# Twenty of 24 head units of a two-block model as seven products each, with sums by GpSimd, and their loads on the weight queue

## What is computed

```python
h = _rmsnorm(x, g_mix_pre)
proj = h @ w_in                                     # 2048 x 16832
q = _rope(proj[..., OFF_DA_Q:OFF_DA_K].reshape(B, S, DA_HEADS, 2, DA_HEAD_DIM), pos)
k = _rope(proj[..., OFF_DA_K:OFF_DA_V].reshape(B, S, DA_HEADS, 2, DA_HEAD_DIM), pos)
v = proj[..., OFF_DA_V:OFF_RW].reshape(B, S, DA_HEADS, DA_V_DIM)
o_a = _diff_attention(q, k, v, lam, da_subln_g, lambda_init)      # 8 heads
o_b = _rwkv7(proj[..., OFF_RW:OFF_GATE], ...)                     # a recurrence in chunks of 64
gates = sigmoid(proj[..., OFF_GATE:] + b_gate)
mix = (gates[..., :D] * (o_a @ w_branch_a) + gates[..., D:] * (o_b @ w_branch_b)) @ w_out
```

## Time and profile before

| | us |
|---|---|
| median of 3 runs | 3943.13 (3942.73 to 3945.35) |
| the profiled execution | 3944.76, of which the span from first to last instruction is 3943.0 |

### The profile page before, as it was taken

How to read it: one execution, slowest core, us unless ns; L and a number is a source line. 1 busy time by engine, 2 the same in 40 slices (tenths; PEclk the granted TensorE clock), 3 DMA queues, 4 the chain that set the end, 5 groups by cost and what they waited for, 6 DMA issues and landing times.

```text
span 3943.0 us, 66861 instructions
## 1 busy us (share of the span) xinstructions
PE 3817.8 (97%) x28964; PEld 3559.2 (90%) x28964; DVE 1799.8 (46%) x3157; ACT 592.8 (15%) x1314; POOL 1308.9 (33%) x737
## 2 busy tenths in 40 slices
PE   8999999999999999999999999989898899999997
PEld 7888888889888999999999998878697899999997
DVE  1344426582223613111135446552522788778544
ACT  0333311110111111000000000232402211111001
POOL 0000000046511774777750000001340677775000
PEclk9999999999999999999999999999999999999999
DMA  6565664447664543444444554427242344444442
GB/s 230 212 217 215 217 231 162 160 166 237 211 196 171 206 161 148 165 165 168 169 166 162 171 193 165 170 108 204 75 169 83 115 172 171 171 171 150 172 159 77
DMA packets 122133, 673.37 MB, mean 171 GB/s; under 512 B 31872, under 2 KB 38144, under 8 KB 91248
## 3 DMA queue, kind: packets, MB, share of 16 engines
q1 hardware_dynamic: 87200, 580.29, 41.0%
q0 software_dynamic: 11104, 42.89, 3.5%
q10 hardware_dynamic: 23536, 45.92, 3.3%
HBM read 615.80 MB, written 53.25 MB: 170 GB/s over the span
## 4 chain that ended last, share of the span: by engine, by line
PE 93%; DVE 3%; ACT 2%; DVEq 1%; issue 1%; ACTq 0%; DMA 0%; POOL 0%; POOLq 0%
PE product_bank L576 53%; PE product_bank L635 26%; PE product_bank L413 3%; PE mixer_bank L784 1%; PE mixer_bank L800 1%; ACT xT L902 0%; PE mixer_bank L1334 0%; PE mixer_bank L1348 0%; PE mixer_bank L1165 0%; PE product_bank L2416 0%; PE mixer_bank L2378 0%; PE mixer_bank L2344 0%; PE mixer_bank L1157 0%; DVE arena L832 0%; PE mixer_bank L1323 0%
## 5 line engine op out<-in xcount | busy, mean ns | idle before, releaser
L635 PE MATMUL product_bank<-hT,weight_ring 128*128 128x256 f32 x2688 | 593.6, 380 | 1.6 <-ACT out_stage L674 1.6
L635 PEld LDWEIGHTS product_bank<-hT,weight_ring 128*128 128x128 f32 x2688 | 508.8, 190 | 75.3 <-issue 7.2
L576 PE MATMUL product_bank<-hT,weight_ring 128*128 128x128 f32 x4160 | 521.9, 276 | 14.5 <-DVEq L1808 5.8
L576 PEld LDWEIGHTS product_bank<-hT,weight_ring 128*128 128x128 f32 x4160 | 494.0, 193 | 20.2 <-DVEq L1808 6.0
L576 PE MATMUL product_bank<-arena,weight_ring 128*128 128x128 f32 x3168 | 394.6, 275 | 0.0
L543 POOL TENSOR_TENSOR arena<-weight_ring 128x1024 f32<-128x1024 f32 x88 | 209.6, 2382 | 528.3 <-PE product_bank L576 284.8
L576 PEld LDWEIGHTS product_bank<-arena,weight_ring 128*128 128x128 f32 x3168 | 374.8, 192 | 0.6
L611 DVE TENSOR_TENSOR arena<-product_bank,arena 128x128 f32<-128x128 f32 x126 | 36.7, 291 | 712.4 <-PE product_bank L576 712.4
L2804 DVE SCALAR_TENSOR_TENSOR arena<-arena 128x256 f32<-128x256 f32 x176 | 320.1, 1857 | 16.5 <-ACT arena L2769 13.2
L546 POOL TENSOR_TENSOR weight_ring<-weight_ring 128x1024 f32<-128x1024 f32 (+1 forms) x142 | 315.5, 2222 | 0.0
L576 PE MATMUL product_bank<-hT,arena 128*128 128x128 f32 x2096 | 257.1, 276 | 1.4 <-DVE hT L532 1.4
(11 more groups left out here) (506 smaller groups left out, 5435.8 us busy)
## 6 DMA issues: line engine op xcount, KB each, us to landing
weight_ring<-in_weights SPq DMA_DIRECT2D x213, 2048.0 KB, 8.0
weight_ring<-in_weights SPq DMA_DIRECT2D x128, 512.0 KB, 5.6
weight_ring<-in_weights SPq DMA_DIRECT2D x64, 384.0 KB, 5.3
units<-out_stage ACTq DMA_DIRECT2D x87, 256.0 KB, 7.7
rwkv_keep<-arena ACTq DMA_DIRECT2D x16, 1282.0 KB, 6.3
arena<-rwkv_keep SPq DMA_DIRECT2D x8, 1280.0 KB, 11.8
arena<-units POOLq DMA_DIRECT2D x33, 256.0 KB, 3.4
arena<-units SPq DMA_DIRECT2D x25, 256.0 KB, 9.0
```

The source lines that it names most:

```text
L576: mm = pe.matmul(bank[:, at * P:at * P + P], lhs[:, j, :], rhs[:, j, :], start=g == 0 and n in (0, 3) and j == 0, stop=g == n_groups - 1 a ...
L635: mm = pe.matmul(psg[b][:, half * T:half * T + T], lhs, rhs, start=k == 0, stop=k == 15)
```

## The change

The head units get two stage names: "heads0" for the first 4, still plain, and "heads" for the other 20, which become sevens in two groups, as the gates' units are. Their weights, their slots and their order stay. A v unit is stored by token, so it takes weights and source in the other places of the matmul (`turned`), and its recombination writes to the quadrants in another order.

GpSimd no longer loads anything for the heads. It waits for the last recurrence tile and sums for 20 + 16 units in one list (`early_sums_pool`), with the same buffers, though the buffers of both groups lie in `yT` for all "heads" units. ScalarE copies one of seven products and stores a unit one unit later, when VectorE has recombined it. VectorE recombines 20 units more, in its program behind the quarters in which a plain unit's would have stood empty.

SP loads the inverse's matrix behind the weights of the ninth head unit and the heads' q, k and v behind those given in `HEAD_LOADS_AT`. The loads of gates unit 4 have nothing behind them any more. The source is combined once, at the same place as before.

```diff
+HEADS_PLAIN = 4
+ORDER += [("heads0", u) for u in range(HEADS_PLAIN)] + [("heads", u) for u in range(24 - HEADS_PLAIN)]
+def turned(name, u):
+    return name in ("heads0", "heads") and head_and_part(name, u)[1] == 2
...
-                if n == UNIT_AT["gates", 4][0]:
-                    last_head_load(sp)
+                if n == UNIT_AT["heads0", 0][0] + 8:
+                    inverse_load(sp)
+                for h in HEAD_LOADS_AT.get(n - UNIT_AT["heads0", 0][0], ()):
+                    head_load(sp, h)
...
-        EARLY = ("gates",)
+        EARLY = ("heads", "gates")
...
+                        one, other = (rhs, lhs) if turned(name, u) else (lhs, rhs)
+                        mm = pe.matmul(bank[:, at * P:at * P + P], one[:, j, :], other[:, j, :],
...
-        def inv_pool(pool):
-            all_kept(pool)
-            pool.dma_start(inv_M, l_units).then_inc(sem("inverse_moved"), 16)
+        def inverse_load(sp):
+            all_kept(sp)
+            sp.dma_start(inv_M, l_units).then_inc(sem("inverse_moved"), 16)
...
-        def gates_sums_pool(pool):
-            for u in range(16):
+        def early_sums_pool(pool):
+            pool.wait_ge(sem("rw1_tile_done"), RW_TILES)
+            for n, unit in enumerate(SEVENTHS):
                 for g in range(2):
-                    if (u, g) == (6, 1):
+                    if (unit, g) == (("gates", BESIDE_DA), 1):
                         pool.wait_ge(sem("attn_head_done"), DA_HEADS)
-                    sum_gates(pool, u, g)
+                    sum_early(pool, n, g)
...
+        HEAD_LOADS_AT = {8: [0], 10: [1], 13: [2], 16: [3], 19: [4], 22: [5], 25: [6], 28: [7]}
+
+        def head_load(sp, h):
+            s = h % 2
+            if h >= 2:
+                sp.wait_ge(sem("attn_head_done"), h - 1)
+            for c in range(3):
+                unit = head_unit(h, c)
+                unit_stored(sp, *unit)
+                sp.dma_start(dain[:, s, c, :], row_of(*unit)).then_inc(sem(f"da_in{s}"), 16)
...
+        SEVENTHS = [("heads", u) for u in range(24 - HEADS_PLAIN)] + [("gates", u) for u in range(16)]
+
+        def sum_early(pool, n, g):
+            if n:
+                group_used(pool, *SEVENTHS[n - 1], g)
+            name, u = SEVENTHS[n]
+            sum_weights(pool, name, u, g, early_sums_of(name, u, g))
...
+        def early_product_act(act):
+            act.wait_ge(sem("rw1_tile_done"), RW_TILES)
+            for n, (name, u) in enumerate(SEVENTHS):
+                yield
+                yield
+                if n:
+                    store_early(act, n - 1)
+                yield
+                if n >= 2:
+                    seq = UNIT_AT[SEVENTHS[n - 2]][1]
+                    act.wait_ge(bank_free[seq % 4], seq // 4 + 1)
+                copy_first_act(act, name, u, gates_first[u % 2])
+                yield
...
+                if turned(name, u):
+                    sides = kept_.rearrange("p (h c n) -> p c h n", h=2, c=2)
+                    left, right = sides[:, 0, :, :], sides[:, 1, :, :]
+                else:
+                    left, right = kept_[:, 0:T], kept_[:, T:2 * T]
+                recombine_dve(dve, name, u, gates_first[u % 2], *gates_temps, left, right)
+                dve.drain().then_inc(sem("early_kept"), 1)
...
             rw1_pool(pool)
-            inv_pool(pool)
-            da_pool(pool)
-            gates_sums_pool(pool)
+            early_sums_pool(pool)
...
-            elsewhere = (None for _ in range(4 * 45))
-            dense = chain(elsewhere, gates_product_dve(dve))
+            elsewhere = (None for _ in PLAIN for _ in range(4))
+            dense = chain(elsewhere, early_product_dve(dve))
```

More of the change, by code:

```diff
@@ L53 @@
 ]
-STORED = ("rkv", "lora", "qk", "v", "gates", "mem_k", "mem_v", "sqk", "sv", "nq", "nkc", "nk", "nv", "ng")
+STORED = ("rkv", "lora", "heads0", "heads", "gates", "mem_k", "mem_v", "sqk", "sv", "nq", "nkc", "nk", "nv", "ng")
 class Stage:
@@ L87, with head_and_part, head_unit @@
 GROUPS = 6
+def head_and_part(name, u):
+    return divmod(u + (HEADS_PLAIN if name == "heads" else 0), 3)
+def head_unit(h, part):
+    k = 3 * h + part
+    return ("heads0", k) if k < HEADS_PLAIN else ("heads", k - HEADS_PLAIN)
+def turned(name, u):
+    return name in ("heads0", "heads") and head_and_part(name, u)[1] == 2
 def plan():
@@ L105, in plan @@
             first = home[name] + (u // shared) * max(1, int(slots))
+            if name in ("heads0", "heads"):
+                h, part = head_and_part(name, u)
+                first = (home["qk"] + h, home["qk"] + 8 + h, home["v"] + h)[part]
             here = len(loads)
@@ L590, in early_quarters @@
             for u in range(PLAN[name].units):
-                steps = unit_sevens(pe, name, u, lambda g: half(source_blocks(src), g), lambda g: sums(u, g),
+                steps = unit_sevens(pe, name, u, lambda g: half(source_blocks(src), g), lambda g: sums(name, u, g),
                                     lambda g: half(combined, g))
@@ L611, in recombine_dve @@
             dve.tensor_tensor(u2, X[:, P:2 * P], first, ALU.add)
-            dve.tensor_tensor(left[:, 0:P], X[:, 0:P], first, ALU.add)
+            left, right = (v if len(v.shape) == 3 else halves(v) for v in (left, right))
+            dve.tensor_tensor(left[:, 0, :], X[:, 0:P], first, ALU.add)
             dve.drain()
@@ L630, in unit_quarters @@
                 for k in range(16):
-                    if st.layout == "T":
+                    if st.layout == "T" and not turned(name, u):
                         lhs, rhs = w[:, k, half * P:half * P + P], src[:, k, :]
@@ L1488, in build @@
         LAM = small[:, 20:22]
[L1490 to L1505, removed]
+        HEAD_LOADS_AT = {8: [0], 10: [1], 13: [2], 16: [3], 19: [4], 22: [5], 25: [6], 28: [7]}
[7 more added lines that the diff above has]
+                sp.dma_start(dain[:, s, c, :], row_of(*unit)).then_inc(sem(f"da_in{s}"), 16)
         def da_head_in(eng, i, s):
[L1508 to L1511, removed]
+            eng.wait_ge(sem(f"da_in{s}"), 48 * i + 48)
         def da_pe(pe):
@@ L2816, in build @@
         RKV_GROUPS = [[("rkv", 8 * c + t) for c in range(3)] for t in range(8)]
-        HEAD_GROUPS = [[("qk", h), ("qk", 8 + h), ("v", h)] for h in range(DA_HEADS)]
+        PLAIN = [unit for group in RKV_GROUPS[1:] for unit in group] + [("heads0", u) for u in range(HEADS_PLAIN)]
         RW1_LEAD, DA_LEAD, RW2_LEAD = 4, 14, 6
@@ L2886, in _ @@
                 run(unit_quarters(pe, name, u, hT))
-            dense = chain(*(unit_quarters(pe, name, u, hT) for group in RKV_GROUPS[1:] + HEAD_GROUPS for name, u in group),
-                          early_quarters(pe, "gates", hT, early_combined, gates_sums_of),
+            dense = chain(*(unit_quarters(pe, name, u, hT) for name, u in PLAIN),
+                          *(early_quarters(pe, name, hT, early_combined, early_sums_of) for name in ("heads", "gates")),
                           quarters(pe, "branch_a", oaT, ready="attn_head_done", count=DA_HEADS))
@@ L2918, in _ @@
                 store_unit(act, name, u)
[L2919 to L2920 removed]
+            dense = chain(*(unit_store_quarters(act, name, u) for name, u in PLAIN), early_product_act(act), branch_a_act(act))
             beside(dense, rw1_act(act), beside_rw1, RW1_LEAD)
@@ L2958, in _ @@
             dve.drain()
-            combine_source_dve(dve, "gates", source_blocks(hT), early_combined)
+            combine_source_dve(dve, "heads", source_blocks(hT), early_combined)
             def heads_and_inverse():
```

45 lines of the change are left out of this document (16 added, 29 removed).

## The result

The changed kernel takes 3994.5 us (median of 4 runs, 3990.07 to 3999.3), the kernel before 3943.5 beside it: a ratio of 1.0127 (1.0115 to 1.0139), 1.3% slower. The forecast was 3975 with a range of 3932 to 4015. The profiled execution took 3995.7 us, its span 3993.8, so 50.8 us of span are to be found. Lines have moved: L576 is now L599 (sevens), L635 L659 (plain), L617 L641 (a recombination's last instruction), L1193 and L1196 (inverse) L1217 and L1220, L1574 L1591, L1581 L1598 (roped k), L1603 L1620 (softmax's last), L1610 L1627, L1524 L1541 (rotation), L1531 L1548 (scores), L1537 L1554 (transposes).

The account below looks back on a forecast made before the run. TensorE, busy 97%, bounds the kernel before; in the changed heads VectorE was to set the pace. From 3944.8 us: +31.5 for seven heads, 0 for lead, head 7 and loads, -1.6 to the median: 3975 us, range 3932 to 4015.

Parts of the forecast that it names:

- The rival that VectorE keeps up: Heads: sums fall into VectorE's rests, TensorE sets the pace; 3917 us, or 3934 with stalls; chance 0.20.
- the one that GpSimd is the bound: Heads: stretched sums take GpSimd 43.4 us a head, so no change, 3943 us; chance 0.09.
- the one of the queue: SP's loads: a head's load waits for a late store, weights behind come late; +54, 3971 us; chance 0.04.
- the forecast had 12: Heads: 12 VectorE instructions a head stretched by GpSimd's sums, 0.91 us each; ends 4 and 22.
- its own 32.3 us: VectorE's own work and short waits in a head before: 43.5 us less 11.2 of rest ahead of the reciprocal.
- the forecast had 48.0: Distance between heads: VectorE's 37.3 us plus 12 collisions of 0.91 is 48.2, rounded to 48.0.
- The price of 0.91: What a VectorE instruction loses beside a GpSimd sum: 1.67 us instead of 0.76 for 572 elements.
- the prediction's 4005 by that rule: Total if each collision cost VectorE a whole sum, 1.27 us and not 0.91: 30 us more.
- +31.5: Seven heads' term: 7 x 48.0 = 336.0 us, before 304.5.
- no term of the sum is about the clock: Lead and heads: the clock stood at 1.00, the upper level, so the sum gives it 0 us.
- 7 or 8: TensorE's lateness a head, in us: some 4 for rope, 2 for softmax, 1 to 2 for ScalarE behind recombinations.
- the 4.6 that was taken: Lead: TensorE's wait for first sums, between 0 and 8 us, taken as +4.6 to even the -4.6 gain.

Follow-up runs that it names:

- idle_sums: Kernel before with the changed loads, all head units plain, GpSimd making 20 units' sums on scratch nobody reads; 3974.5 us, ratio 1.0078.
- short_sums: Changed kernel with the head units' sums over 16 columns instead of 128 of each block; 3939.3 us, one run.
- loads_only: Kernel before with the inverse's and all heads' loads on SP, head units plain, no GpSimd sums in that stage; 3944.3 us, ratio 1.0001.
- placed: Changed kernel with VectorE's inverse steps only behind the softmax and its neighbours, none between reciprocal and rope; 3992.3 us, ratio 1.0121.
- early_inverse: Changed kernel with the first 8 head units plain and 20 of the inverse's 62 steps done in the lead; 3959.6 us, ratio 1.0040.
- front_inverse: Changed kernel with 12 head units plain, 20 inverse steps in the lead, 16 more in heads beside plain units; 3943.7 us, ratio 0.9999.
- front_placed: front_inverse with the inverse steps left for heads beside sums placed only behind the softmax; 3950.4 us, ratio 1.0015.
- placed8: early_inverse with the other 42 inverse steps placed only behind the softmax; 3960.1 us, ratio 1.0042.
- front_placed_after: front_placed with the inverse steps behind the recombination due at a head's step instead of ahead of it; 3936.1 us, ratio 0.9980.

## Why the prediction was right and wrong

**Direction and mechanism: right.** VectorE became what TensorE waits for, through the stretch of its own instructions and the recombinations. `idle_sums` shows the first without the second, `short_sums` the second without the first, and without the stretch the seven heads beat the old ones. The rival that VectorE keeps up is out (46 to 53 us apart, not 40 to 42). So are the one that GpSimd is the bound (TensorE waits 1.3 us for it) and the one of the queue (`loads_only`). The Trainium skill, Perfetto Trace Analysis, section Identifying the Most-Contended Engine, would have the engine with the highest occupancy relieved first, TensorE here (97%, and 90% by its weight loads, which is the measure that the page prefers). The runs show that the relief of 1.31 us a unit is lost when an engine that is busy 46% gets it as work in a fixed order.

**The account of a head: its terms right, its sum partly luck.** The seven heads have 92 stretched instructions, 13.1 a head, which cost 12.0 us; the forecast had 12, at 10.9. With its own 32.3 us and 5.0 of recombinations that gives 49.3, and the distances from rope to rope on VectorE have a mean of 49.8; the forecast had 48.0, and TensorE's rotations stood 48.8 apart. But the 32.3 is misread. Of the seven rests of 78.7 us one, 13.0 us, is head 7's; the last head beside the inverse had none. The seven heads have 65.7 us of such rests, and the 34 us a head that this leaves already hold 21 stretched instructions (20.0 us, 2.9 a head) and two recombinations. Over the five heads that had neither, VectorE's own work and short waits are 43.3 - 12.0 = 31.3. And VectorE didn't stand in the way all the time afterwards: it still rested 17.8 us ahead of the reciprocal, 2.5 a head, while short waits for TensorE's products (14.6 us before, none now) fell away. These errors nearly cancel. The price of 0.91 held from 180 to 990 elements. GpSimd's sums in the seven heads (form, count, busy us, mean ns), forecast at 1.5 us or more:

```profile
L568 POOL TENSOR_TENSOR weight_ring<-weight_ring 128x512 f32<-128x512 f32 x39 | 65.5, 1680 | 0.0
L567 POOL TENSOR_TENSOR yT<-yT,weight_ring 128x512 f32<-128x512 f32 x39 | 62.0, 1589 | 5.5
L570 POOL TENSOR_TENSOR yT<-yT,weight_ring 128x512 f32<-128x512 f32 x38 | 58.7, 1546 | 5.4
L565 POOL TENSOR_TENSOR yT<-weight_ring 128x512 f32<-128x512 f32 x39 | 55.6, 1425 | 94.2 <-PE product_bank L599 94.2
```

Their mean is 1.56 us, against 1.27 alone; single ones beside the inverse took up to 2.2, more than the 1.73 to 1.84 of the prediction. The Trainium skill, SBUF — State Buffer, section Who interferes with whom, has the one engine block fully until the other's instruction is over. Each stretched instruction of VectorE lost less than a whole sum here, 0.91 of 1.27 us, and the 3994 that came lies nearer to the prediction's 4005 by that rule for other reasons, the clock above all.

**The seven heads: +38.5 instead of +31.5.** The step that failed is "no term of the sum is about the clock". The waits were 6.2 us a head, less than the "7 or 8" that was said: 2.4 for the rope where some 4 stood, 1.9 for the softmax where 2 stood, 1.7 for recombinations where 1 to 2 stood. The other 2.6 us a head are TensorE's own work at the lower clock, which the kernel before had no reason to show: it hardly waited there. That is also the larger part of why its busy time rose by 4.6 us and did not fall by 26; the rest is the lead and the late stage below. The granted clock was 0.90 to 0.96 in six heads with waits, and 1.00 before. The Trainium skill, TensorE: Matmul & The Clock Gate, section HAM oscillation — how this bites in real kernels, has this effect: where the engine waits again and again, products behind each wait start at the lower clock, and that is a cost beside the wait. The trace agrees, with 18.2 us beside 43.2 of waits. It is a rule that spoke against the change and was not weighed.

**The lead: +4.3 instead of 0.** The first two sums, on GpSimd in the changed kernel, and TensorE's first product with them:

```profile
520.47 1.26 POOL L565 TENSOR_TENSOR yT<-weight_ring 128x512 f32<-128x512 f32 x1 [48.94 <-DVEq L1087]
527.61 1.26 POOL L567 TENSOR_TENSOR yT<-yT,weight_ring 128x512 f32<-128x512 f32 x1 [5.88 <-issue]
528.83 1.26 POOL L568 TENSOR_TENSOR weight_ring<-weight_ring 128x512 f32<-128x512 f32 x1
```

```profile
531.64 2.05 PE L599 MATMUL product_bank<-hT,weight_ring 128*128 128x128 f32 x8 [5.79 <-POOL yT L570]
```

The gap between first and second sum, 7.7 us where it was seen before, came again with 5.9, and TensorE stood 5.8: nearer to the upper of the two ends, 0 and 8, than the 4.6 that was taken. Behind it 8 records took 2.05 us instead of 1.06, and the stage's clock of 0.94 over 55.35 us is worth up to 3.3 more. The wait for head 0's rotation is 1.6 where it was 0.8: -4.6 + 5.8 + 3.3 + 0.8 = 5.3 at most, 4.3 measured.

**Head 7: right,** 42.6 as before. **The rest of the kernel: not foreseen.** Of the last 8 us little arises in the next 1700: the same instructions of TensorE stand 42.4 us later at 2060 us, 44.2 at 2660, and 50.4 at 2820 (48.9 from 2860 on), in the attention of block 2. One table row there for the kernel before, and then one for the changed kernel, over nearly the same work:

```profile
2770.00:2870.00 100.00, 88.89 (x511) 70.32 (x511) 48.17 (x144) 38.10 (x145) 28.64 (x25) 0.95 0.21 74
```

```profile
2815.00:2915.00 100.00, 88.91 (x474) 69.55 (x473) 48.05 (x140) 38.09 (x145) 28.19 (x24) 0.91 0.21 71
```

The code is the same and the longer waits are alike, but the clock is 0.91 and not 0.95, up to 4 us in 100. Runs of the changed kernel also spread over 9 us, those of the one before over 3. The stretch of the sums is not needed for it: in the trace of `short_sums` the same instructions fall back by 6 us in the same place, at a clock of 0.92 as in the changed kernel, where the kernel before has 0.95 (its 2660 to 2820 us). In `placed` they fall back by 3 us, and in the ten other traces by less than 1 in the end. So some 7 of the 50.8 us are not shown to be a cost of the stretched instructions. Why a stage 1900 us later should get another clock in some executions was not tried, and it stays open.

**The forecast as a whole** fell 19.5 us short: about 7 in the seven heads (336.0 against 341.9, and a base that begins 1.1 us too soon), 4.3 in the lead, and 8 behind the heads. Its range also takes the 1.6 us to the median off twice: 45 and 54 us a head give 3954 and 4017.

**In the experiments** five expectations failed. `idle_sums` (3974.5, expected 3948 to 3962) counted only stalls and missed the clock and part of the waits. `early_inverse`, `front_inverse`, `front_placed` and `placed8` all came out above the time expected for them. In the first two the load was taken for the whole cause: it is, as long as VectorE has no room (`placed` moves the waits, and its 3992.3 us lies within the runs of the changed kernel), but below that the order decides (8 and 14 us between kernels with the same work). In the two after them the place was taken for enough, and the recombination behind it was overlooked. What load and order each cost in `early_inverse` and `placed8` was not taken apart further.

## What to carry to other kernels

Before GpSimd gets additions with both inputs in SBUF, count VectorE's instructions of that kind beside them and put about 0.9 us on each that will meet a sum, whatever its size (here 92 of 160 did); compare that engine's work in a period, not its share of the span, with the period of the engine to be relieved. Give such sums only to stretches where VectorE has room, and put work that another engine waits for (here the recombination) ahead of filler work in its queue. If TensorE has run without a gap, count its new waits of several microseconds by more than their length: here 43.2 us of waits came with some 18 us of slower products. In the other kernels with such waits the seven heads' length times what their clock lacked was 0.2 to 0.6 of the waits (20.1 us of waits and 10.1 in `idle_sums`, 8.5 and 1.7 in `front_placed_after`).

## What the runs showed of the hardware

- A collision costs VectorE about 0.9 us, and that doesn't grow with its own instruction, from 180 to 990 elements; GpSimd's sums of 1.27 us took 0.3 us more in the mean over all of them. L1617, with one SBUF input, was lengthened too: 0.28 to 0.35 us alone, 0.9 to 1.4 for five of the 14 in the seven heads.
- TensorE's granted clock fell in stretches where it had waited several microseconds at a time, in a kernel that keeps it busy 96%. Eight records took 2.05 us right behind such a wait, 1.06 elsewhere, as fits 1.2 and 2.4 GHz.
- GpSimd's second sum came 5.9 us after its first had ended (7.7 in the kernel before), with nothing in the trace that it waited for; the third began as the second ended (528.83).
